# A decoder trunk on one core: one hardware queue for the weight chunks and the modulation weights

## What is computed

```python
cond = jax.nn.silu(c)                                   # (1, 1024)
for l in range(DEPTH):                                  # 2 layers
    if l == N_A_LAYERS:                                 # before layer 1
        kv_mod = (cond @ w_kv_ada + b_kv_ada).reshape(b, 2, d)
        kv = modulate(x, kv_mod[:, 0], kv_mod[:, 1]) @ w_kv_b
    mod = (cond @ w_ada[l] + b_ada[l]).reshape(b, 9, d)  # shift, scale, gate x 3
    h = modulate(x, mod[:, 0], mod[:, 1])
    x = post_norm_residual(x, swiglu(h, w_ffn_in[l, 0], w_ffn_out[l, 0]), mod[:, 2], 0.5, ...)
    h = modulate(x, mod[:, 3], mod[:, 4])
    ...                                                 # layer 0: QKV, rotary, softmax attention
    ...                                                 # layer 1: Q, stick-breaking attention on kv
    x = post_norm_residual(x, y, mod[:, 5], 1.0, ...)
    h = modulate(x, mod[:, 6], mod[:, 7])
    x = post_norm_residual(x, swiglu(h, w_ffn_in[l, 1], w_ffn_out[l, 1]), mod[:, 8], 0.5, ...)
```

## Time and profile before

| | |
|---|---|
| median of 3 runs | 1090.98 us (1090.12 to 1091.12) |
| span of the profiled execution | 1088.1 us |
| TensorE busy | 97% |
| VectorE busy | 72% |
| ScalarE busy | 47% |
| GpSimd busy | 5%, its DMA issues |
| moved by the hardware queue of SyncE | 183.13 MB |
| moved by the software queue of GpSimd | 75.53 MB |

### The profile page before, as it was taken

One profiled execution on the slowest core, in us unless ns is written; L12 is line 12 of the kernel. 1 busy time (PEld: TensorE's weight loads), 2 busy tenths in 40 slices (PEclk: granted clock), 3 DMA queues, 4 the chain that ended last, 5 costly groups with the idle time before them and its releaser, 6 DMA issues.

```text
span 1088.1 us, 18522 instructions
## 1 busy us (share of the span) xinstructions
PE 1052.3 (97%) x7269; PEld 959.2 (88%) x7279; DVE 785.8 (72%) x869; ACT 515.5 (47%) x822; POOL 54.9 (5%) x82
## 2 busy tenths in 40 slices
PE   3999999999999999999999999999999999999996
PEld 1799999978898899999979999999979779999995
DVE  7687778789864886768785577777789676544576
ACT  1644543463464644543464554444455664444333
POOL 0000001100000000001100001000100000000000
PEclk9999999999999999999999999999999999999999
DMA  9999999948744399999948399999967537665631
GB/s 358 325 345 351 323 314 291 353 148 267 275 117 120 105 306 310 297 314 290 348 151 232 118 297 291 300 310 288 333 228 231 195 87 223 193 192 170 186 147 39
DMA packets 248730, 265.76 MB, mean 244 GB/s; under 512 B 7273, under 2 KB 212457, under 8 KB 248681
## 3 DMA queue, kind: packets, MB, share of 16 engines
q1 hardware_dynamic: 226848, 183.13, 55.1%
q0 software_dynamic: 19776, 75.53, 19.4%
q10 hardware_dynamic: 2056, 6.42, 1.7%
HBM read 264.01 MB, written 1.05 MB: 244 GB/s over the span
## 4 chain that ended last, share of the span: by engine, by line
PE 92%; DVE 3%; ACT 3%; DMA 1%; issue 1%; DVEq 0%; SPq 0%
PE psum L1081 20%; PE psum L1082 20%; PE psum L1083 20%; PE psum L1189 9%; PE psum L1190 9%; PE psum L1191 9%; PE psum L1120 1%; PE psum L1128 1%; PE psum L1308 1%; DMA raw<-in_w_ada 1%; DVE tmp L734 1%; DVE acc L734 1%; PE psum L1111 1%; ACT tmp L478 1%; ACT h_full L478 1%; PE psum L1261 1%
## 5 line engine op out<-in xcount | busy, mean ns | idle before, releaser
L1081 PE MATMUL psum<-hT_hi,w_hi 128*128 128x256 f32 x1664 | 475.5, 286 | 2.9 <-DVE hT_lo L833 1.7
L1083 PE MATMUL psum<-hT_hi,w_lo 128*128 128x256 f32 x1664 | 471.6, 283 | 0.0
L1082 PE MATMUL psum<-hT_lo,w_hi 128*128 128x256 f32 x1664 | 471.5, 283 | 0.0
L702 DVE TENSOR_TENSOR w_lo<-raw,w_hi 128x2048 fp32r<-128x2048 f32 x164 | 375.2, 2288 | 125.6 <-ACT w_hi L408 125.6
L408 ACT ACTIVATE w_hi<-raw 128x2048 fp32r<-128x2048 f32 x164 | 313.0, 1909 | 111.0 <-PE psum L1191 109.8
L1081 PEld LDWEIGHTS psum<-hT_hi,w_hi 128*128 128x128 f32 x1664 | 319.0, 192 | 13.7 <-issue 4.3
L1082 PEld LDWEIGHTS psum<-hT_lo,w_hi 128*128 128x128 f32 x1664 | 319.1, 192 | 1.0
L1083 PEld LDWEIGHTS psum<-hT_hi,w_lo 128*128 128x128 f32 x1664 | 319.0, 192 | 0.0
L734 DVE SCALAR_TENSOR_TENSOR acc<-ada,cond,acc 128x1024 f32<-128x1024 f32 x130 | 166.6, 1282 | 9.3 <-DMA ada<-in_w_ada 5.8
L413 ACT ACTIVATE tmp<-psum 128x256 f32<-128x256 f32 x88 | 33.7, 383 | 278.4 <-PE psum L1083 278.4
L1189 PE MATMUL psum<-w_hi,a_hi 128*128 128x512 f32 x352 | 139.2, 396 | 0.0
(11 more groups left out here) (154 smaller groups left out, 837.3 us busy)
## 6 DMA issues: line engine op xcount, KB each, us to landing
raw<-in_w_ffn_in SPq DMA_DIRECT2D x176, 512.0 KB, 6.0
ada<-in_w_ada POOLq DMA_DIRECT2D x64, 1024.0 KB, 5.7
raw<-in_w_ffn_out SPq DMA_DIRECT2D x88, 512.0 KB, 5.2
raw<-in_w_qkv_a SPq DMA_DIRECT2D x24, 512.0 KB, 6.5
raw<-in_w_o SPq DMA_DIRECT2D x16, 512.0 KB, 5.6
ada<-in_w_kv_ada POOLq DMA_DIRECT2D x8, 1024.0 KB, 6.2
raw<-in_w_kv_b SPq DMA_DIRECT2D x16, 512.0 KB, 6.4
raw<-in_w_ada SPq DMA_DIRECT2D x6, 1024.0 KB, 11.0
```

Source lines behind the costliest of these rows:

```text
L702: nc.vector.tensor_tensor(w_lo[:, n % SPL, :], raw[:, n % RAW, :], w_hi[:, n % SPL, :].bitcast(F32), ALU.subtract).then_inc(w_lo_ready, 1)
L1081: nc.tensor.matmul(dst, s_hi, m_hi, start=start, stop=False)
L1082: nc.tensor.matmul(dst, s_hi, m_lo, start=False, stop=False)
L1083: return nc.tensor.matmul(dst, s_lo, m_hi, start=False, stop=stop)
```

## The change

`load_unit` and the whole GpSimd program go. SyncE issues the quarters and the gate biases too, from its own hardware queue, in one order with the chunks. A table `taken` says how many quarters VectorE has used by the time it splits a given chunk. After each chunk n, `refill(n)` looks up how many quarters are used by the split of chunk n - 6, for which `load` has just waited, and issues quarters up to two beyond that. `load_quarter` still waits for `acc_steps`. SyncE's loops over FFN steps are written out, since the table differs from step to step. The code of the other engines is unchanged.

```diff
+        taken = {}
+        for f in range(4):
+            steps = [(1 + 2 * b + i, ((1, 1, 0))) for b in range(LOOPS) for i in range(2)] if FIRST_UNIT[f] is not None else []
+            for s, counts in steps + [(STEPS - 2, (2, 1, 1))]:
+                for i in range(3):
+                    taken[N_FFN[f] + 3 * s + 2 + i] = counts[i]
+        for i in range(2, 6):
+            taken[N_QKV + i + 3] = 1
+        taken[N_Q + 4] = 2
+        taken[N_WO[1] + 1] = 2
+
         @block.sync
         def _(sp):
...
+            filled = [4 * (STAGED // 4)]
+
+            def load_quarter(u, q):
...
+                sp.wait_ge(acc_steps, 8 * u + 2 * q - 2)
+                sp.dma_start(ada[:, q % 2, :, :], ada_view(w)[:, 2 * q:2 * q + 2, j * D:(j + 1) * D])\
+                    .then_inc(ada_in[q % 2], 16)
+
+            def refill(n):
+
+                done = 4 * (STAGED // 4) + sum(c for m, c in taken.items() if m <= n - RAW)
+                while filled[0] < min(done + 2, 4 * UNITS):
+                    load_quarter(filled[0] // 4, filled[0] % 4)
+                    filled[0] += 1
+
+            def load(n, halves):
+
+                if n >= RAW:
+
+                    sp.wait_ge(w_lo_ready, n - RAW + 1)
...
+                if n >= RAW - 1:
+                    refill(n)
...
             load_ffn(3)
+            refill(N_ALL + RAW)
...
-        @block.gpsimd
-        def _(pool):
-            def load_unit(u):
...
-                for q in range(4):
-
-                    pool.wait_ge(acc_steps, 8 * u + 2 * q - 2)
-                    pool.dma_start(ada[:, q % 2, :, :],
```

More of the change, by code:

```diff
@@ L294, in build @@
                 [(N_Q + i, w_q_b[0], 256 * i) for i in range(4)])
+        taken = {}
[8 more added lines that the diff above has]
+        taken[N_WO[1] + 1] = 2
         @block.sync
         def _(sp):
-            def load(n, halves, at=None):
-                if at is not None or n >= RAW:
-                    sp.wait_ge(w_lo_ready, n - RAW + 1 if at is None else at + (n - RAW + 1))
+            filled = [4 * (STAGED // 4)]
+            def load_quarter(u, q):
+                layer, j = ORDER[u]
+                w, b = (w_kv_ada, b_kv_ada) if layer == KV else (w_ada[layer], b_ada[layer])
+                if u in GATE_OF and q == 0:
+                    g = GATE_OF.index(u)
+                    if g:
+                        sp.wait_ge(acc_steps, 8 * GATE_OF[g - 1] + 1)
+                    else:
+                        sp.wait_ge(set_up, 1)
+                    sp.dma_start(bias0[0:1, :], b[j * D:(j + 1) * D].rearrange("(a n) -> a n", a=1))\
+                        .then_inc(bias_in, 16)
+                sp.wait_ge(acc_steps, 8 * u + 2 * q - 2)
[9 more added lines that the diff above has]
+                    sp.wait_ge(w_lo_ready, n - RAW + 1)
                 else:
@@ L308, in load, with load_step @@
                     sp.dma_start(dst.rearrange("p (k n) -> p k n", n=src.shape[2]), src).then_inc(raw_in[n % RAW], 16)
[L310 to L315, removed]
+                if n >= RAW - 1:
+                    refill(n)
+            def load_step(w_in, w_out, n, s):
+                load(n + 3 * s - 1, inner_chunk(w_in, 256 * s))
+                load(n + 3 * s, inner_chunk(w_in, (256 * s + P)))
+                load(n + 3 * s + 1, rows_chunk(w_out, 256 * (s - 1)))
             def load_ffn(f):
@@ L320, in load_ffn @@
                 load(n + 1, inner_chunk(w_in, P))
-                peeled = 2 if f == 0 else 0
-                for s in range(1, 1 + peeled):
+                for s in range(1, STEPS):
                     load_step(w_in, w_out, n, s)
[L325 to L330, removed]
+                    if f == 0 and s == 2:
+                        sp.dma_start(cst[:, P:], consts[:, P:]).then_inc(cst_in, 16)
                 load(n + FFN_CHUNKS - 1, rows_chunk(w_out, DFF - 256))
```

## The result

The changed kernel takes 1116.53 us, the median of 4 runs (1115.91 to 1119.98), against 1090.82 (1090.12 to 1091.12) for the kernel before beside it. The ratio is 1.0246, interval 1.0233 to 1.0258: 2.5% slower. The forecast was 1108.9 with a range from 1101 to 1115. The sign and the chain of waits at the gate steps are as forecast; the loss is 25.7 us where 17.9 was expected, a loss at the start was not forecast at all, and the time lies 1.5 us outside the range. The span of the profiled execution is 1115.2 us, 27.1 more than before.

A forecast was written before the change was run, and what follows sets the result against it. TensorE, busy 97%, was taken to bound the kernel, so its new waits add in full: 11.7 (waits) + 5.1 (clock) + 1.1 (stick-breaking) = 17.9 us on 1088.1, 1106.0, plus 2.9 outside the span: 1108.9 us, range 1101 to 1115.

The forecast's parts named there:

- the tight place: Gate step, step 9 of the FFNs, taking four quarters (Q0 to Q3): a late quarter holds VectorE, then `w_lo`, then TensorE.
- The term of the wait: Gate steps of FFN 0 to 2: TensorE waits 3.9 us each, 11.7 us in all; bounds 7.5 to 19.
- Q2 lands at T + 7.6: Gate step: the third quarter lands 7.6 us after T, its release at the split of n+29; bounds T + 6.2, T + 10.1.
- Q1: Gate step's second quarter, behind chunk n+33: lands 7.6 us after that split ends, before it is wanted; costs 0 to 0.4.
- The clock: After each of the three gate-step waits TensorE's clock falls, losing 1.7 us: 5.1 in all; bounds 0 and 5.1.
- Rival 1: Gate steps: same waits but no fall of TensorE's clock, 1103.8 us; chance 0.17.
- The stick-breaking stage: Q2 and Q3 of that gate leave behind chunk N_Q+10, delaying `hT_lo`: +1.1 us, from 0 to 3.
- The 2.9 us "for work outside the span": Whole kernel: the median of the runs shown, 1090.98, lies 2.9 us above the profile's span; added to the forecast.
- The sign "some 25 us": VectorE's waits for `ada` grow from 5.8 to some 25 us, in three blocks of about 7 at gate steps.
- Rival 2: Gate steps: transfers served side by side, Q2 landing with Q3, 6.4 us of wait each, 1118.3 us; chance 0.08.
- Rival 3: Gate steps: not slower, Q2 lands in time or the place of issue does not matter, 1091.0 us; chance 0.06.
- rival 4: Start: faster, first FFN chunks land sooner without Q0 and Q1 beside them; at most 1.1 us, 1089.9; chance 0.03.

The follow-up runs named there:

- experiment 2: The changed kernel with `refill` moved ahead of the chunk's wait for `w_lo`, so a quarter waits only for `acc_steps`: 1090.16 us against 1090.50, ratio 0.9997.
- experiment 6: The changed kernel with `refill` ahead of the wait only at chunk n+35 of FFN 0, 1 and 2: 1093.94 us against 1090.97, ratio 1.0041.
- experiment 7: The changed kernel, but at the gate steps of FFN 0, 1 and 2 Q3 is issued only when Q2 has landed: 1118.66 us, ratio 1.0257.
- experiment 8: The changed kernel with `refill` ahead of the wait only at chunks 11 and 12, the first loop steps of FFN 0: 1116.09 us, ratio 1.0237.
- experiment 5: The changed kernel with 20 products of zeros per FFN ahead of chunk n+30 in FFN 0, 1 and 2, inside the new wait: 1111.72 us, ratio 1.0206.
- experiment 3: The changed kernel with `refill` between the wait for `w_lo` and the chunk's two halves, so the quarter goes ahead of the chunk: 1094.94 us, ratio 1.0040.
- experiment 1: The kernel before with SyncE's loops written out and GpSimd still issuing the quarters: 1090.16 us against 1090.50, ratio 0.9998.

## Why the prediction was wrong in size and right in kind

In spans the loss is 27.1 us against the 17.9 of the sum. The 9.2 us between them are 4.8 of waits, 1.7 of clock, 2.6 at the start and 0.1 in the stick-breaking stage.

- **What bounds the kernel, and the tight place: right.** TensorE has new waits, and the large ones are three waits for `w_lo` of n+30, with nothing given back later (experiment 2 returns to the time before, experiment 6 removes 22.6 us at three chunks).
- **The term of the wait, 3 x 3.9 = 11.7 us: mis-sized**, 16.5 measured. The step that failed is "Q2 lands at T + 7.6". VectorE could use it at T + 8.44, 8.6 and 9.4. The sum put the landing of a chunk alone and the bare transfer of a quarter one behind the other. In the trace the second half of the chunk lands 4.7 us after 208.3, at 213.0, as assumed, but Q2 only at 216.2, that is 3.2 us later instead of 2.6. In gate step 0 the 0.84 us of Q2 and 0.3 by which T itself is late make 5.04 out of 3.9. In gate step 1 it is the 1.0 of Q2. In gate step 2 Q2 is 1.8 late, and T another 0.9, because Q1 was 1.05 late. All three landings are within the bound of T + 10.1, so the mechanism and its bounds held, and the value taken between them was too near the lower end. Q3 is excluded as the cause (experiment 7). What its trace shows in place of a bare transfer is a slow end: the last 0.1 MB took 1.3 us. Why the last pieces of Q2 come so late stays open.
- **Q1, counted among what costs nothing, with "0 to 0.4": too narrow.** It was 0.43, 0 and 1.05 us late in the changed kernel, 2.54 in experiment 8 and 2.81 in experiment 6. In gate step 0 it landed 9.3 us after its issue at 193.7, so 10.3 behind its release where 7.6 was put; the LayerNorm rows that the prediction named were under way too, 1.05 MB on another queue between 187 and 205. In gate step 2 it adds to TensorE's wait in full.
- **The clock, 3 x 1.7 = 5.1 us: right in kind, too small.** The fall follows each wait; experiment 5 takes it away. The step that failed is the row it was sized by: 3.4 us at half speed at the start, taken as value and as upper bound at once. In gate step 0 the low level lasted 6.2 us. The three losses are 2.9, 1.6 and 2.3, together 6.8. A single row gives no upper bound. Nor was the start a like case: there 1.9 us of idle time were followed by the low level, while behind the new wait of 2.21 us at 87.83 the granted clock stayed at 1.00. Rival 1 (no fall) is refuted here; in experiment 3, where the waits are 1.2 us, there is indeed no fall.
- **The stick-breaking stage, 1.1 us: right**, 1.2 measured.
- **The start, counted at nothing: this step was missing.** The loop was tested with one place in the steady state, where a quarter has 3.9 us to spare, and no loss appeared there. But the first moved quarters are issued while the start's loads are still being worked off, and there one landed after 11.0 us. That is 2.6 us; with it in the sum the forecast would have been 1111.5.
- **The 2.9 us "for work outside the span": misread.** The runs whose spans are known lie about 1.8 us above them; the other 1.1 is that the profiled execution before was faster than the median. The forecast does not change, since it adds the loss to the median.
- **The sign "some 25 us" of VectorE's waits for `ada`: 35.4 measured.** The three blocks at the gate steps are 24.4 of it; the start, Q1, the QKV stage (once, 0.80, which did not reach TensorE) and the stick-breaking stage are the rest.
- **FFN 3, the QKV stage, the loop, the unrolling and the removal of GpSimd's issues: right, no cost.** FFN 3 shows no wait for a quarter; the shift does not grow between 237.15 and 524.47; experiment 1 measured the unrolling at 0.9998.
- **Rival 2** (Q2 and Q3 served side by side, T + 10.1, 1118.3) is near in time, but not in mechanism: Q2 lands at 216.2 and Q3 at 220.3, 4.1 us apart. The two overlap by some 0.5 MB, but holding Q3 back did not help (experiment 7). **Rival 3**, with the rule that the issuing engine makes no difference, is half true: moving all issues to one queue costs nothing once the order is right (experiment 2, 0.9997). The Trainium skill, "DMA: Bandwidth & Descriptors", section Issuing engines are not separate DMA queues, says as much about the transfers themselves. It speaks of the issue time alone as what several issuers save; here a second issuer also saved the wait that an in-order program puts ahead of a transfer, and that was 25.7 us. What rival 3 says of the time, not slower, is refuted, and so is rival 4, faster.

No version tried beats the kernel before. Experiment 2 equals it with GpSimd free.

## What to carry to other kernels

When two streams of transfers are merged into one issuer's program, each transfer is released by the later of its own event and all waits written ahead of it. So place it ahead of the other stream's next wait, and look for the irregular steps (a step that takes more buffers than the others, the start while its loads are under way), not at the loop. A buffer's refill should wait for the event that frees it. A proxy a few microseconds later costs whatever exceeds the time in hand: 4.6 us later meant 1.2 us of wait at each gate step here with the quarter first, and 4.9 to 6.6 us once 1 MB of another transfer stood ahead of it. And where TensorE is the bound, a new wait of about 5 us has a second price, the clock behind it, of 1.6 to 2.9 us here; one of 1.2 us had none.

## What was not expected of the hardware

- After idle times of 5.0, 4.9 and 6.6 us TensorE lost 2.9, 1.6 and 2.3 us to the clock. The loss does not follow the length of the idle time. After 2.2 us of idle time at 87.8 and 1.2 us in experiment 3 it lost nothing.
- The issue of one transfer on SyncE took 0.37 to 0.5 us at gate step 0, and 4.48 (68.01) or 8.20 us (68.19, experiment 8) when the start's loads were still under way. The quarter issued at 68.01 landed after 11.0 us.
- 1 MB of quarter landed 4.9 us after its issue with nothing ahead of it (experiment 3), and 7.4 us after it behind 1 MB of chunk issued just before.
- Of the 2.1 MB of a chunk and a quarter the last 0.1 MB took 1.3 us, at 85 GB/s (experiment 7).
